# Attention rounds of a two-stack transformer kernel: the turn of the second head placed between the value products of the two heads

## What is computed

```
s = q @ k.T * scale + mask_or_bias        # 256 x 256, in two row blocks of 128
p = exp(s - max(s))                       # not divided yet
o = (p @ [v, 1])                          # 64 columns of values, 1 column of sums
out = o[:, :64] / o[:, 64:]               # and a gate, where the layer has one
```

## Time and profile before

| | us |
|---|---|
| median of three runs (lowest, highest) | 998.48 (997.11, 998.93) |
| the profiled execution | 998.88 |
| its span in the profile | 997.1 |
| TensorE busy | 957.4 |
| VectorE busy | 646.0 |
| ScalarE busy | 470.8 |
| GpSimd busy | 179.8 |
| granted TensorE clock, mean over the span | 0.997 |

### The profile page before, as it was taken

How to read it: one execution, slowest core, us unless ns; L and a number is a source line. 1 busy time by engine, 2 the same in 40 slices (tenths; PEclk the granted TensorE clock), 3 DMA queues, 4 the chain that set the end, 5 groups by cost and what they waited for, 6 DMA issues and landing times.

```text
span 997.1 us, 15096 instructions
## 1 busy us (share of the span) xinstructions
PE 957.4 (96%) x5662; PEld 807.1 (81%) x5662; DVE 646.0 (65%) x1158; ACT 470.8 (47%) x729; POOL 179.8 (18%) x152
## 2 busy tenths in 40 slices
PE   5999899989999999999999999999999999999996
PEld 2799566768886789888888888879999888888885
DVE  3656567875664775666776666676346676766665
ACT  1453577535545645573444444444447344444442
POOL 2015137203970401050000000010014000000001
PEclk9999999999999999999999999999999999999998
DMA  9864555434565246223365655534532336555541
GB/s 373 354 232 167 211 211 190 150 128 169 188 223 199 86 158 242 98 85 127 128 231 210 210 210 189 189 122 184 202 111 101 127 128 238 187 191 189 191 183 42
DMA packets 24104, 178.37 MB, mean 179 GB/s; under 512 B 3791, under 2 KB 4223, under 8 KB 7927
## 3 DMA queue, kind: packets, MB, share of 16 engines
q1 hardware_dynamic: 19840, 166.70, 45.2%
q0 software_dynamic: 2224, 8.94, 2.9%
q10 hardware_dynamic: 1991, 2.07, 0.7%
HBM read 176.65 MB, written 1.05 MB: 178 GB/s over the span
## 4 chain that ended last, share of the span: by engine, by line
PE 85%; DVE 9%; ACT 2%; DMA 2%; issue 1%; POOL 0%; SPq 0%; DVEq 0%; ACTq 0%; POOLq 0%
PE G L1082 14%; PE G L1084 14%; PE G L1083 14%; PE S L1202 8%; PE T L1202 8%; PE S L1201 3%; PE T L1201 3%; PE T L606 2%; PE T L511 2%; PE G L616 1%; PE G L615 1%; PE G L614 1%; DMA early<-in_ada_w 1%; PE G L431 1%; DVE wlo L2094 1%
## 5 line engine op out<-in xcount | busy, mean ns | idle before, releaser
L2225 DVE TENSOR_TENSOR wlo<-ring,whi 128x2048 fp32r<-128x2048 f32 x88 | 154.4, 1758 | 88.5 <-ACT whi L1796 55.2
L1082 PE MATMUL G<-whi,hTh 128*128 128x512 f32 (+3 forms) x560 | 196.7, 351 | 4.2 <-DVE oTl L552 2.0
L1083 PE MATMUL G<-wlo,hTh 128*128 128x512 f32 (+3 forms) x544 | 186.1, 342 | 0.0
L1084 PE MATMUL G<-whi,hTl 128*128 128x308 f32 (+3 forms) x496 | 167.3, 337 | 0.0
L2094 DVE TENSOR_TENSOR wlo<-ring,whi 128x1024 fp32r<-128x1024 f32 (+3 forms) x66 | 105.4, 1633 | 64.0 <-ACT whi L1656 63.7
L1202 PE MATMUL S<-hT,whi 128*128 128x512 f32 x336 | 122.1, 397 | 0.0
L1202 PE MATMUL T<-hT,whi 128*128 128x512 f32 x336 | 120.7, 394 | 0.0
L1082 PEld LDWEIGHTS G<-whi,hTh 128*128 128x128 f32 x560 | 105.2, 188 | 18.8 <-issue 5.7
L1083 PEld LDWEIGHTS G<-wlo,hTh 128*128 128x128 f32 x544 | 102.4, 188 | 7.8 <-issue 0.7
L1084 PEld LDWEIGHTS G<-whi,hTl 128*128 128x128 f32 x496 | 93.3, 188 | 5.7
L1791 ACT CAST whi<-ring 128x2048 fp32r<-128x2048 f32 x44 | 83.9, 1906 | 25.0 <-PE S L1278 17.6
(11 more groups left out here) (376 smaller groups left out, 1834.4 us busy)
## 6 DMA issues: line engine op xcount, KB each, us to landing
ring<-in_ffn SPq DMA_DIRECT2D x44, 1536.0 KB, 6.4
ring<-in_dil_w_in SPq DMA_DIRECT2D x16, 1024.0 KB, 4.8
ring<-in_cd_w_in SPq DMA_DIRECT2D x10, 1232.0 KB, 5.3
ring<-in_ada_w SPq DMA_DIRECT2D x12, 1024.0 KB, 6.6
early<-in_ada_w SPq DMA_DIRECT2D x8, 1024.0 KB, 9.9
ring<-in_nsa_w_in SPq DMA_DIRECT2D x5, 1432.0 KB, 6.0
ring<-in_ab_w_in SPq DMA_DIRECT2D x4, 1440.0 KB, 6.3
vec<-in_vecs POOLq DMA_DIRECT2D x11, 512.0 KB, 5.1
```

The source lines that it names most:

```text
L1082: pe.matmul(out_, act_h, w_h, start=first_, stop=False)
L1083: pe.matmul(out_, act_h, w_l, start=False, stop=False)
L1084: return pe.matmul(out_, act_l, w_h, start=False, stop=last_)
L2225: TT(wlo[b][:, part], ring[:, b, part], whi[b][:, part].bitcast(F32), ALU.subtract).then_inc(st[what + "_lo"], 1)
```

## The change

In rounds in which pairs are in all three steps (2 <= p < pairs) the turn of the second head of pair p - 1 moves behind `behind(p)`, the wait for the eviction, and the value product of the first head of pair p - 2. The order on TensorE was: scores, turn, turn, `behind`, value product, value product. It is: scores, turn, `behind`, value product, turn, value product. Rounds 0, 1, pairs and pairs + 1 keep their order, and so does every other engine.

```diff
                 if 1 <= p < pairs + 1:
-                    for j in (2 * p - 2, 2 * p - 1):
-                        turn_probs(j)
+                    turn_probs(2 * p - 2)
+                    if p < 2 or p == pairs:
+                        turn_probs(2 * p - 1)
                 if p == pairs:
                     times_v(2 * p - 3)
                 if behind is not None:
                     behind(p)
                 if p >= 2 and p != pairs:
                     if p >= 3:
 
                         pe.wait_ge(att["outs"], b0 // 2 + min(p, pairs) - 2)
-                    for j in (2 * p - 4, 2 * p - 3):
-                        times_v(j)
+                    times_v(2 * p - 4)
+                    if p < pairs:
+                        turn_probs(2 * p - 1)
+                    times_v(2 * p - 3)
                 if after is not None:
                     after(p)
```

## The result

The changed kernel takes 1001.17 us (median of six executions, 1001.08 to 1001.75), the kernel before 997.95 (six, 997.11 to 998.93). The ratio is 1.0032, with an interval of 1.002 to 1.0044: 3.2 us slower. The forecast was 1000.6, which is 2.1 us above the 998.48 that was the median of the kernel before when it was made.

What follows compares the result with a forecast made beforehand. TensorE, busy 957.4 of 997.1 us, was taken as the bound. Waits +1.6 and collision +1.1 less 0.6 for cheaper switches gave +2.1 us: 1000.6 against the median of 998.48, range 998.0 to 1002.0.

Steps and rivals of the forecast that it cites:

- Part 2: In "nsa" rounds 2, 6, 7, 9, 11 and 13, turns moved behind waits of the side work are paid for: +1.6 us.
- part 3: Behind round 6 of "nsa", VectorE's later multiplication falls inside GpSimd's second addition and is held: 1.1 us more loss.
- The collision: VectorE's L2494 starting inside GpSimd's L965 behind round 6, by 0.04 us: 1.1 us; rival without it 999.5 us, chance 0.27.
- the two readings of the port: VectorE and GpSimd's shared port: exclusive lock gives the sum with 1.1 us, sharing in time the one without.
- The output projection: Its first product, behind "nsa", takes over the shift; if it doesn't, the prediction is wrong.
- Part 1: Switches between turns and products in 32 changed rounds: 0.05 us gained each, 0.6 us taken in all, bounds 0 and 1.6.
- The moved waits: Waits for the eviction and ScalarE's second copy around the moved turn: put at nothing, the copy covered by 1.1 us.
- The wait for the eviction: In "dil", ahead of the first value product: ready with 0.05 us to spare, costed at nothing, otherwise 0.3 us.
- slower still: Rival: one more collision in "nsa" up to 1.1 us, 1001.7, or the eviction wait bites, with "dil" 1002.0; chance 0.08.

Runs made afterwards that it cites:

- e8: The kernel before with the new order only in rounds 7, 9, 11 and 13 of "nsa"; 999.79 us, ratio 1.0014.
- e3: The kernel before with the new order in round 6 of "nsa" alone, all three transposes late; 1000.87 us, ratio 1.0026.
- e4: The kernel before with only the last two of the second head's three transposes moved, in round 6 of "nsa" alone; 998.51 us, ratio 1.0002.
- e7: The changed kernel with the old order in every round `pairs` - 1 and in "nsa" rounds 2, 4, 6, 7, 9, 11, 13; 997.8 us, ratio 0.9992 against before.
- e5: The changed kernel with the old order kept in round `pairs` - 1 of each attention; 1000.16 us, ratio 1.0021 against the kernel before.
- e1: The kernel before with the new order in "nsa" alone; 1001.02 us, ratio 1.003.
- e10: The kernel before with the reciprocal of the "nsa" eviction written to PSUM, order unchanged; 997.96 us, ratio 0.9993.
- e2: The kernel before with the new order in "dil", "ab" and "cd" but not in "nsa"; 998.73 us, ratio 1.0005.
- e6: The changed kernel with the old order in round 6 of "nsa"; 999.75 us, ratio 1.0015 against the kernel before.
- e9: The changed kernel with the reciprocal of the "nsa" eviction written to PSUM; 999.5 us, ratio 1.0009 against the kernel before.
- e11: The changed kernel with the reciprocal in PSUM, old order in each round `pairs` - 1 and "nsa" rounds 2, 4, 6, 7; 996.97 us, ratio 0.9986 against before.
- e12: The changed kernel with ScalarE's copies behind the exponentials in round `pairs` - 1 too; 1005.04 us, ratio 1.0058 against the kernel before.

## Why the prediction was right, and where it fell short

**The direction and the mechanisms of "nsa" held.** Part 2 gave +1.6 us and part 3 +1.1, 2.7 at the scores of round 14; the trace has 2.69. Two small misses cancel in it: round 6 costs 0.32 instead of 0.27, and round 5 gives back 0.05 that wasn't counted. Each step has its row. Round 2: 1.31 - 0.97 = 0.34 more idle time for a turn of 0.33. Round 6: 0.34 us ahead of L1444. Rounds 9, 11 and 13: 0.35, 0.34 and 0.35 us ahead of L431, put down to L2490 (the row of round 9 is below); with round 7, e8 priced the four at 1.14 where 1.12 stood. The collision came from a margin of 0.05 us, and e3 and e4 showed that it is a threshold. Of the two readings of the port, the exclusive lock is what the traces show: the held instruction ends with the L968 (142.68 and 142.66), and moving one operand out of SBUF removes the wait (160 to 163 ns in all 16). The rule of the Trainium skill's page "SBUF — State Buffer", section "SBUF: two separate sides", says the same of a VectorE instruction with two inputs in SBUF, and these numbers agree with it. The output projection took over the whole shift. Timeline of after, PE, round 9:

```profile
153.41 1.06 PE L431 MATMUL G<-ring,cb 128*32 128x512 f32 x8 [0.35 <-DVE tmp L2490]
```

**Part 1 had the right size and missed a term.** 0.05 us a round is what "cd" shows, and e7, less the collision in "dil", gains 0.6 us by the stages. The step that failed is in "The moved waits": "ScalarE's second copy needs the moved turn ... and the cover is 1.1 us". The 1.1 us were read in round 4 of "dil" and taken for every round. In round `pairs` - 1 the copies stand ahead of the exponentials, the cover is nothing, and the second copy waits 0.47 us in "cd". The transposes of the next round take 1.24 us instead of 0.82 in "cd", and 1.23 or 1.24 in "ab", "dil" and "nsa". e5 put it at 0.46 us in "ab" and 0.51 in "cd". In "dil" it is 0.14 of the 0.34 that e5 gave back; the other 0.20 is a collision (below). In "nsa" it is 0.20, which accounts for the 0.16 us that the changed kernel lost between the scores of round 14 and the output projection: in e5 these are gone. That makes 1.3 us in all. With it, the other three attentions do not win 0.6 but lose 0.29 by the stages (-0.21 + 0.22 + 0.28), and this and the 0.16 of "nsa" are the 1.05 us by which the stages exceed the forecast. The condition stands in `att_act`; the prediction followed only its usual branch.

**"dil" came out near its number by luck: errors that cancel.** The wait for the eviction, costed at nothing with 0.05 us to spare, does bite. Timeline of after, PEld, the weight load at the end of "cd"; then PE, PEld and DVE in round 4 of "dil":

```profile
773.37 0.30 PEld L614 LDWEIGHTS G<-u,probT 128*128 128x128 f32 x2
...
326.72 0.44 PE L614 MATMUL G<-u,probT 128*128 128x65 f32 x2
...
327.77 0.33 PE L614 MATMUL G<-u,probT 128*128 128x65 f32 x2
...
326.72 0.30 PEld L614 LDWEIGHTS G<-u,probT 128*128 128x128 f32 x2
...
325.81 0.86 DVE L2171 SCALAR_TENSOR_TENSOR tok<-G,rden,u 128x64 f32<-128x64 f32 x4
```

The eviction ends at 325.81 + 0.86 = 326.67, and the weight load of the first value product starts at 326.72, together with the product, where it otherwise stands 0.1 us ahead of it (773.37 for 773.48 in "cd"). The product is 0.44 us instead of 0.33. So a wait of almost no length goes with a loss of 0.1 us; that the load can't go ahead is the reading that fits the two rows. Rounds 4, 5 and 6 all show it and take 3.01, 3.00 and 3.00 us, where those of "cd" take 2.90: the 0.3 us that the prediction named for this wait, should it bite, though it had six rounds of 0.05 in mind and these are three of 0.1. Against that stands a gain that wasn't seen: a sum of VectorE with two inputs in SBUF (L2586 of before) collides with GpSimd's L1013 at the end of "dil". Timeline, DVE, of before, of after and of e7:

```profile
335.25 1.07 DVE L2586 TENSOR_TENSOR lse<-glse,negmax 128x32 f32<-128x32 f32 x1
```

```profile
337.17 0.81 DVE L2589 TENSOR_TENSOR lse<-glse,negmax 128x32 f32<-128x32 f32 x1
```

```profile
334.07 0.63 DVE L2589 TENSOR_TENSOR lse<-glse,negmax 128x32 f32<-128x32 f32 x1
```

It lasts until GpSimd's instruction ends, so the later in it it starts, the less it costs: 0.26 us came back in after and 0.44 in e7. GpSimd's row of this work starts when its weights have come by DMA (322.53 us in before), not by the rounds, so which part of it VectorE meets is luck. The record shows how the -0.21 us divides. "dil" less the length of this one sum takes 31.45 to 31.47 us in all six kernels with the old order there (before, e1, e3, e4, e8 and e10), 31.51 to 31.60 in those with the new order in all its rounds (after, e2, e6 and e9), and 31.36 or 31.37 in e5, e7 and e11, which keep the old order in the last one. So the order itself costs "dil" 0.05 us in after, and the rest of the -0.21 is the collision; without round `pairs` - 1 the order gives 0.09 us.

**The chances.** The case that came true is "slower still" in its size: the loss is 3.2 us, which was its price for one more collision (1001.7), with the mechanism of the forecast in "nsa" and an unnamed one at the end of the rounds. The range of 998.0 to 1002.0 holds 1001.17. That this stands only 0.6 above the forecast of 1000.6 flatters it: the kernel before, measured beside the changed one, took 997.95 and not 998.48, and the loss came out 1.1 us larger than the 2.1 forecast.

## What to carry to other kernels

A step moved behind a wait costs its whole length, since it was work that the wait got for nothing: look for idle time in the rows directly behind the place that it leaves. When an instruction is moved inside a software pipeline, price the first and the last round one by one, because there the other engines' order is often another one. An instruction of VectorE with two inputs in SBUF, beside long GpSimd work, was a threshold of a microsecond here; writing one operand to PSUM took it away.

## What the runs showed of the hardware that was not expected

TensorE's clock can fall in or just behind an idle gap of about a microsecond, in some executions and not in others. Stretches of after and of e12 (us, busy time and instructions of each engine, granted clock, DMA share, GB/s):

```profile
144.00:146.00 2.00, 2.00 (x18) 1.16 (x19) 1.74 (x9) 1.43 (x4) 1.22 (x1) 1.00 1.00 422
146.00:147.00 1.00, 1.00 (x9) 0.83 (x8) 0.18 (x1) 1.00 (x3) 0.87 (x1) 1.00 1.00 426
```

```profile
144.00:146.00 2.00, 1.56 (x8) 0.16 (x8) 1.58 (x9) 0.91 (x3) 1.28 (x1) 0.64 1.00 418
146.00:147.00 1.00, 1.00 (x8) 0.75 (x4) 0.63 (x1) 1.00 (x3) 0.35 (x1) 0.50 0.95 401
```

And TensorE's row behind the gap in e12, where the same eight products take 1.06 us in after:

```profile
144.44 1.89 PE L431 MATMUL G<-ring,cb 128*32 128x512 f32 x8 [1.41 <-DVE tmp L2487]
```

Ahead of L431 of round 7 TensorE was idle for 1.40 us in after and kept its full clock of 2.4 GHz; in e12, which up to round 14 runs the same program, it was idle for 1.41 us and was at half of it, 1.2 GHz, from just behind the start of L431 until shortly before 148 us. From the scores of round 7 to those of round 8 it took 40.46 - 32.35 = 8.11 us instead of 38.82 - 32.34 = 6.48, so 1.6 us more. Of e12's five executions, two have a mean granted clock of 0.998 over the span (1003.32 and 1003.75 us) and three have 0.996 (1005.04 to 1005.32). e3 is divided in the same way: four executions with 0.997 or 0.998 at 999.07 to 1000.25 us, four with 0.995 at 1001.50 to 1002.10. That puts e3's median about 1.2 us above the +1.4 that its stages say.

Whether the fall lies behind round 6 in e3's slower executions isn't shown; the profiled execution of e3 was one at full clock. There is a rival, for the clock can fall elsewhere, at a place that the change doesn't touch. Stretches and timeline (PE) of e8, whose profiled execution has a mean clock of 0.995, behind "dil":

```profile
343.00:344.00 1.00, 0.16 (x2) 0.00 (x0) 0.78 (x2) 1.00 (x4) 0.00 (x0) 0.90 0.00 0
344.00:345.00 1.00, 0.94 (x2) 0.83 (x3) 0.90 (x2) 1.00 (x2) 0.00 (x0) 0.50 0.00 0
```

```profile
344.06 0.76 PE L1085 MATMUL G<-whi,hTh 128*128 128x512 f32 x1 [0.90 <-DVE oTl L552]
```

The kernel before has the same idle time of 0.90 us there and keeps its full clock. From the end of "dil" to the first scores of "ab" e8 takes 83.01 us, where the other thirteen profiled executions take 81.54 to 81.61. Nor does the mean clock alone tell the loss: e6 has three executions with 0.995 or 0.996 that take 999.52 to 999.75 us, no longer than its other eight (999.59 to 1001.22). The mean also holds the end of the span, where the clock is low in each of the kernels (0.57 from 990 us on in before, whose mean is 0.997). What decides which execution loses its clock, and where, stays open.
